# Five units of the second layer's input projection made ahead of a stage boundary and kept in PSUM

## The chip, the cores and the metric

The kernel runs on one core of a Trainium2 chip. The metric is the device time of one launch in microseconds (us); lower is better. The core has TensorE (PE, the matrix products), VectorE (DVE), ScalarE (ACT), GpSimd (POOL) and SyncE (SP, which here only issues transfers). Each runs its own list of instructions in order, and they wait for each other by semaphores. Matrix products are written to PSUM, which has 8 banks of 512 float32 numbers per partition; the other data lie in SBUF.

## The reference

One inference step of a two-layer decoder over 1024 prompt positions and 8 sequences of 8 new positions, 1088 columns in all. Layer 0 has mixers A and B, layer 1 the mixers C and D, and each layer ends with a SwiGLU block. The change lies where layer 0 ends and layer 1 begins:

```python
# end of layer 0
h = rmsnorm(x, norm_ffn_pre) * (1 + sc_f) + sh_f
f = swiglu(h, w_gate, w_up, w_down)          # (silu(h @ wg) * (h @ wu)) @ wd
x = x + g_f * rmsnorm(f, norm_ffn_post)
# start of layer 1
h = rmsnorm(x, norm_mix_pre) * (1 + sc_m) + sh_m
proj = h @ w_in
a, g, u, v = jnp.split(proj, [D_C, 2 * D_C, 2 * D_C + D_D], axis=-1)
hist = jnp.concatenate([conv_hist, a * jax.nn.sigmoid(g)], axis=1)
yc = causal_dwconv(hist, conv_w) + conv_b     # 31 taps per channel
yc = jax.nn.silu(layernorm(yc, ln_c_g, ln_c_b))
v = layernorm(v, ln_v_g, ln_v_b)
yd = chunk_spatial(u, v, w_sp, b_sp, chunk_rows)   # u * (tril(w_sp) @ v + b_sp)
y = jnp.concatenate([yc, yd], axis=-1) @ w_out
```

## The kernel before, in words

**Layout.** Activations lie with their features on the 128 partitions, as 8 blocks `d` or `k` of 128 features, and their 1088 columns in four quarters `q` of 272 (the last one has 208 prompt columns and the 64 new positions). A float32 product is made as three products: each operand is split into a high part (a copy in the type fp32r, by ScalarE) and a low part (the difference, by GpSimd or VectorE). `HS[:, 0]` and `HS[:, 1]` hold these parts of the input of the next projection. A weight tile of 1024 x 128 is loaded into a raw buffer by SyncE, copied to its high half by ScalarE (`to_hi`) and split by GpSimd (`to_lo`). A **unit** is one tile times one quarter: 24 products of 272 columns into one bank of PSUM.

**Stages.** The program is a row of stages with a barrier of all engines between them. In each, every engine's instructions are written out by hand in the order of a few loops over units; semaphores with counts tie them together. Of the stages two matter here.

`stage_tail` holds the output projection, the SwiGLU block and the residual additions of a layer. At its end, for layer 0 (`nxt` is set), the four quarters pass through: `close(q)` on TensorE (down products, and `add_f` summing squares of the result), `root_y` (ScalarE) and `invert_y` (VectorE) for the row scale, `scale_one(q, k)` (VectorE: f times gate and row scale; two operations in the last quarter), `add_x(1, q, i)` (GpSimd adds x from `x_part`, which SyncE reloads from `x_spill`, two buffers in turn), `square_x` (ScalarE), `sum_pair` and `fold` (VectorE), `sum_x` (TensorE), `root_x`, `invert_x`, `scale_x(q, k)` (VectorE), `scaled_high(q, k)` (ScalarE, two operations) and `low(q, k)` (GpSimd). The last three fill `HS` for layer 1 in a ring of four buffers `h_next`. The new positions are scaled and split by themselves at the very end (`samples_high`, `samples_low`). `sg` holds the gated products until the last `up`, whose low part raises `hid_lo`.

`stage_cd` is the C/D mixer. TensorE goes through the units `CD_UNITS`: numbers 0 to 7 are tiles `g` and `a` of the first 128 features, for quarters 0 to 3 in turn; 8 to 31 the other three pairs of tiles, four quarters each; then 9 token units (`v`, four tiles at once), 9 spatial units and 16 units `u`. A unit `n` goes to bank `n % 5` and waits until unit `n - 5` has been read: `g` by a sigmoid on ScalarE, `a` by `take_a` on VectorE, which multiplies it with the sigmoid's result. The causal convolution of group `j` is shared out: VectorE adds up `TAPS_V` of the 31 taps (`step`, in banks 6 and 7, two halves), ScalarE multiplies the others (`product`) and GpSimd adds them (`add`). They are spread over the units by the functions

```python
def steps_by(n):
    if n < 16:
        return max(0, min(steps_of[1], 4 * (n - 3)))
def products_by(n):
    if n < 16:
        return max(0, n - 7)
```

so VectorE takes its first four taps at its place `n == 4`, and ScalarE its first product at `n == 8`; both wait for the `take_a` of the quarters that they read. ScalarE makes the first four tiles' high halves before anything else. The spatial weights are turned by TensorE into banks 6 and 7 (`turn_spatial`, at unit 2), masked by VectorE (`mask`), repeated and summed (`row_sums`, unit 3), and set (`row_bias`), all ahead of the first tap.

## Time and profile before

| | |
|---|---|
| median of 3 runs | 3329.01 us (3327.11 to 3336.29) |
| the profiled execution, own time | 3332.6 us |
| its span in the trace | 3330.3 us |
| PE busy | 3086.1 us, 93% |
| DVE busy | 1459.2 us, 44% |
| ACT busy | 1073.5 us, 32% |
| POOL busy | 1064.2 us, 32% |
| mean granted TensorE clock | 0.963 of full speed |

The profile comes from one execution. Its times count from the start of its span; the time of the execution itself is 2.3 us longer than the span. An engine's share of busy time is a mean over stages in which different engines set the pace. The barrier that the change concerns lies at about 2092 us.

### The profile page before, as it was taken

The numbers are of one execution on the slowest core, as the hardware profiler recorded it, in microseconds if no ns is written. First come the engines' busy times: TensorE is split into PE (matmuls) and PEld (weight loads), VectorE is DVE, ScalarE is ACT, GpSimd is POOL, SyncE is SP. The second block draws the span as 40 slices with busy tenths as digits, with TensorE's granted clock in tenths as the row PEclk, the third lists the DMA queues.
The fourth block names the chain that finished last, engine by engine and source line by source line (L and its number), as shares of the span: only waits on it lengthen the run. The fifth ranks groups of instructions, "written<-read, shape, count | busy, mean of one in ns | idle before, by whom it ended". The sixth has DMA issues, their size and how long they took to land. (4 is left out here: it accounts for less than half of the span.)

```text
span 3330.3 us, 60742 instructions
## 1 busy us (share of the span) xinstructions
PE 3086.1 (93%) x24355; PEld 2794.2 (84%) x24355; DVE 1459.2 (44%) x2815; ACT 1073.5 (32%) x2114; POOL 1064.2 (32%) x684
## 2 busy tenths in 40 slices
PE   6999899899999889999999995788889999999997
PEld 4888566677766889999999994777889999999997
DVE  4332355344433563333333358586365333333335
ACT  4411146344443442111111125475553111111113
POOL 2410167333332543221221114477543222211212
PEclk8999989899999999999999997898899999999999
DMA  8555100355554332111111112211222111111103
GB/s 301 174 185 176 53 1 1 130 170 166 170 165 127 92 93 70 44 43 39 38 50 44 44 41 74 74 32 30 77 75 87 47 42 41 44 44 38 50 26 101
DMA packets 237865, 274.98 MB, mean 83 GB/s; under 512 B 12666, under 2 KB 185595, under 8 KB 237428
## 3 DMA queue, kind: packets, MB, share of 16 engines
q1 hardware_dynamic: 215532, 192.60, 18.5%
q0 software_dynamic: 20992, 75.51, 7.1%
q10 hardware_dynamic: 1168, 4.46, 0.4%
q8 instruction: 121, 1.98, 0.2%
q14 instruction: 52, 0.43, 0.0%
HBM read 248.64 MB, written 24.26 MB: 82 GB/s over the span
## 5 line engine op out<-in xcount | busy, mean ns | idle before, releaser
L511 PE MATMUL ps<-HS,w_ring 128*128 128x272 f32 x4992 | 646.9, 291 | 20.6 <-PEq L156 14.8
L511 PEld LDWEIGHTS ps<-HS,w_ring 128*128 128x128 f32 x4992 | 638.5, 190 | 22.2 <-POOLq L905 15.0
L511 PE MATMUL ps<-HS,w_split 128*128 128x272 f32 x4608 | 595.4, 291 | 14.8 <-POOL w_split L880 14.8
L511 PEld LDWEIGHTS ps<-HS,w_split 128*128 128x128 f32 x4608 | 589.5, 190 | 16.0 <-issue 12.9
L519 PE MATMUL ps<-hid,w_ring 128*128 128x272 f32 x4224 | 552.1, 291 | 2.9 <-DVE hid L1063 2.9
L519 PEld LDWEIGHTS ps<-hid,w_ring 128*128 128x128 f32 x4224 | 539.0, 189 | 7.0 <-DVE hid L1063 3.4
L880 POOL TENSOR_TENSOR w_ring<-w_raw,w_ring 128x1024 fp32r<-128x1024 f32 x92 | 219.4, 2397 | 828.5 <-ACT w_ring L621 828.5
L1138 DVE TENSOR_TENSOR Y<-Y,ps 128x272 f32<-128x272 f32 x576 | 252.2, 438 | 176.8 <-PE ps L519 176.8
L621 ACT ACTIVATE w_ring<-w_raw 128x1024 fp32r<-128x1024 f32 x92 | 94.6, 1053 | 471.0 <-PE ps L519 448.7
L1644 PEld LDWEIGHTS ps<-HS_in,w_split 128*128 128x128 f32 x1728 | 222.4, 191 | 27.6 <-issue 16.1
L1054 DVE TENSOR_TENSOR sg<-sg,ps 128x272 f32<-128x272 f32 x176 | 76.4, 437 | 385.3 <-ACT sg L708 385.2
L1644 PE MATMUL ps<-HS_in,w_split 128*128 128x272 f32 x1728 | 233.3, 294 | 9.2 <-DVE HS_in L1863 9.1
L880 POOL TENSOR_TENSOR w_split<-w_raw,w_split 128x1024 fp32r<-128x1024 f32 x46 | 111.2, 2419 | 359.4 <-ACT w_split L621 359.4
L2336 POOL DMA_INDIRECT pages_ckv<-cache_ckv_in,ckv_rows x128 | 120.1, 938 | 289.1 <-PE ps L2408 267.8
L712 ACT ACTIVATE hid<-sg 128x272 fp32r<-128x272 f32 x176 | 75.9, 431 | 413.3 <-DVE sg L1059 413.3
L1059 DVE TENSOR_TENSOR sg<-sg,ps 128x272 f32<-128x272 f32 x176 | 77.1, 438 | 257.0 <-PE ps L511 256.0
L708 ACT ACTIVATE sg<-ps 128x272 f32<-128x272 f32 x176 | 69.1, 397 | 332.8 <-PE ps L511 325.1
L2753 PE MATMUL ps<-HS,w_ring 128*128 128x272 f32 x1152 | 150.0, 293 | 22.3 <-POOL w_ring L2990 22.3
L2753 PEld LDWEIGHTS ps<-HS,w_ring 128*128 128x128 f32 x1152 | 148.0, 191 | 24.0 <-POOL w_ring L2990 23.1
L1063 DVE TENSOR_TENSOR hid<-sg,hid 128x272 fp32r<-128x272 f32 x176 | 115.3, 655 | 88.3 <-ACT hid L712 88.3
L897 POOL TENSOR_TENSOR Y<-Y,x_part 128x544 f32<-128x544 f32 x64 | 97.7, 1532 | 160.4 <-DVE Y L988 116.9
L2355 PEld LDWEIGHTS ps<-cst,pages_ckv 128*128 128x128 f32 x1024 | 112.9, 143 | 35.8 <-DMA pages_ckv<-cache_ckv_in,ckv_rows 29.1
(367 smaller groups left out, 4020.4 us busy)
## 6 DMA issues: line engine op xcount, KB each, us to landing
w_mod_half<-w_mod_in SPq DMA_DIRECT2D x40, 1024.0 KB, 6.9
w_raw<-w_ffn_gate_in SPq DMA_DIRECT2D x44, 512.0 KB
w_raw<-w_ffn_up_in SPq DMA_DIRECT2D x44, 512.0 KB
w_raw<-w_ffn_down_in SPq DMA_DIRECT2D x44, 512.0 KB
x_part<-x_spill SPq DMA_DIRECT2D x64, 272.0 KB, 3.0
x_spill<-Y SPq DMA_DIRECT2D x12, 1088.0 KB, 5.5
w_raw<-w_in_ab_in SPq DMA_DIRECT2D x18, 512.0 KB, 14.6
w_raw<-w_in_cd_in SPq DMA_DIRECT2D x16, 512.0 KB
```

The costliest lines, as they stand in the source:

```text
L511: ins = pe.matmul(bank(b), wt[:, a, k, :], HS[:, e, k, qs(q)], start=(k == 0 and j == 0), stop=(k == KD - 1 and j == 2))
L519: ins = pe.matmul(bank(b), slots[1 + f][:, a, d * P:(d + 1) * P], hid[:, e, f, qs(q)], start=(f == 0 and j == 0), stop=(f == 1 and j == 2))
L621: act.activation(slots[slot][:, 0, :], raw[u][:, :], ACT.Copy).then_inc(w_hi, 1)
L880: pool.tensor_tensor(slots[slot][:, 1, :], raw[u][:, :], slots[slot][:, 0, :].bitcast(F32), ALU.subtract).then_inc(w_lo, 1)
L897: pool.tensor_tensor(y, y, xc[:, 2 * (i % 2):2 * (i % 2) + 2, :], ALU.add).then_inc(x_added, 1)
L1059: dve.tensor_tensor(sg[:, qs(q)], sg[:, qs(q)], bank(b), ALU.mult).then_inc(gated, 1)
L1063: dve.tensor_tensor(hid[:, 1, f, qs(q)], sg[:, qs(q)], hid[:, 0, f, qs(q)].bitcast(F32), ALU.subtract).then_inc(hid_lo, 1)
L1138: dve.tensor_tensor(Y[:, d, qs(q)], Y[:, d, qs(q)], bank(b), ALU.add).then_inc(freed_dve, 1)
L1644: ins = pe.matmul(bank(n), wt[:, a, k, :], HS[:, e, k, qs(q)], start=(k == 0 and j == 0), stop=(k == KD - 1 and j == 2))
L2336: pool.indirect_dma_start(pg[g % NPB][:, e, :, :].rearrange("p a r -> p (a r)"), None, ckv_blocks, bass.IndirectOffsetOnAxis(c.ckv_rows[:, ...
L2355: ins = pe.transpose(CT_[e][:, k, j * P:(j + 1) * P], pg[u][:, e, j, k * P:(k + 1) * P], c.ident)
L2753: ins = pe.matmul(bank(n)[:, 0:Q], weights(t % 4, a, k), HS[:, e, k, qs(q)], start=(k == 0 and i == 0), stop=(k == KD - 1 and i == 2))
```

## The change

Five of the units of `stage_cd`, numbers 0 to 4 (`g` and `a` of the first features for quarters 0 and 1, and `g` for quarter 2), are made at the end of the first `stage_tail`, in banks 0 to 4, and left there over the barrier. For this the first two tiles of `w_in_cd` are loaded into `sg` one after the other once it is free, and split by ScalarE (`ahead_high`) and GpSimd (`ahead_low`) into slots 0 and 3 of the ring of weights; the order of slots in `stage_cd` becomes 0, 3, 2, 1. In `stage_cd` every engine counts these units and tiles as done and starts with tile 2 and unit 5. The spatial weights are turned in two halves at units 16 and 19, in bank 5, and set at 22 and 25. In the tail VectorE does all `scale_one` of the last quarter ahead of the `scale_x` of the one before it, half of which move behind the last `fold`; GpSimd does its additions of x ahead of the splits; and the last quarter's `HS` is made with one operation on ScalarE (`next_high`) and the split on VectorE (`low_next`). The second layer's tail has `nxt` unset and keeps its order.

```diff
--- before.py
+++ after.py
@@ stage_tail, SyncE
                 if nxt:
                     store_x(1, q)
+                if nxt and q == 1:
+                    sp.wait_ge(computed, U.final(3, 3) + 1)
+                    sp.wait_ge(hid_lo, HEND + 8)
+                    for u in range(2):
+                        if u:
+                            sp.wait_ge(a_lo, u)
+                        sp.dma_start(ahead_raw.rearrange("p (k n) -> p k n", k=KD), w_ahead[u]).then_inc(a_in[u], 16)
@@ stage_tail, TensorE
+            def ahead(n):
+                q, u = n // 2, n % 2
+                pe.wait_ge(a_lo, u + 1)
+                pe.wait_ge(h_lo, 33 + 8 * q + 8)
+                if n == 0:
+                    pe.wait_ge(freed_dve, U.END - U.P1)
+                wt = slots[ahead_slot[u]].rearrange("p a (k n) -> p a k n", k=KD)
+                for k in range(KD):
+                    for j, (a, e) in enumerate(((0, 0), (0, 1), (1, 0))):
+                        ins = pe.matmul(c.ps[:, n, 0:Q], wt[:, a, k, :], HS[:, e, k, qs(q)], start=(k == 0 and j == 0),
+                                        stop=(k == KD - 1 and j == 2))
+                ins.then_inc(ahead_done, 1)
+
             if nxt:
+                ahead(0)
                 sum_x(1, 2)
+                for n in range(1, 4):
+                    ahead(n)
                 sum_x(1, 3)
+                for n in range(4, CD_AHEAD):
+                    ahead(n)
+                pe.wait_ge(ahead_done, CD_AHEAD)
@@ stage_tail, ScalarE
+            def ahead_high(u):
+                act.wait_ge(a_in[u], 16)
+                act.activation(slots[ahead_slot[u]][:, 0, :], ahead_raw, ACT.Copy).then_inc(a_hi, 1)
+
                 if nxt:
                     root_x(1, q - 2)
+                if nxt and q == 3:
+                    ahead_high(0)
                 for d in range(KD):
                     square_f(q - 1, d)
                     if nxt:
                         scaled_high(q - 2, d)
+            def next_high(k):
+                layer, part, shift = nxt
+                act.wait_ge(h_made, 32 + 24 + k + 1)
+                act.activation(HS[:, 0, k, 3 * Q:NPR], h_next[k % 4][:, 0:QP], ACT.Identity,
+                               bias=c.mod[:, NM * layer + shift + k, 0:1]).then_inc(h_hi, 1)
+
+            if nxt:
+                ahead_high(1)
             for d in range(KD):
                 square_f(3, d)
@@
+            root_y(1, 3)
             if nxt:
                 root_x(1, 2)
-            root_y(1, 3)
-            if nxt:
-                scaled_high(2, 0)
                 for i in range(4):
-                    for k in range(2 * i + 1, min(2 * i + 3, KD)):
-                        scaled_high(2, k)
                     square_x(1, 3, i)
+                for k in range(4):
+                    scaled_high(2, k)
                 root_x(1, 3)
+                for k in range(4, KD):
+                    scaled_high(2, k)
                 for k in range(KD):
-                    scaled_high(3, k)
+                    next_high(k)
@@ stage_tail, GpSimd
+                if nxt and q == 1:
+                    ahead_low(0)
                 if nxt and q < 2:
                     for k in range(KD):
                         low(q, k)
+                if nxt and q == 1:
+                    ahead_low(1)
             for i in range(4):
-                if nxt:
-                    low(2, 2 * i)
-                    low(2, 2 * i + 1)
                 add_x(1, 3, i)
             if nxt:
                 for k in range(KD):
-                    low(3, k)
+                    low(2, k)
@@ stage_tail, VectorE
-                invert_x(1, 2)
             invert_y(1, 3)
             for k in range(KD):
-                if nxt:
+                scale_one(3, k)
+                if nxt and k == 5:
+                    invert_x(1, 2)
+            if nxt:
+                for k in range(4):
                     scale_x(2, k)
-                scale_one(3, k)
-            if nxt:
                 for i in range(1, 4):
                     sum_pair(1, 3, i)
                 fold(1, 3)
+                for k in range(4, KD):
+                    scale_x(2, k)
                 invert_x(1, 3)
-                for k in range(KD):
-                    scale_x(3, k)
+                make_next(0)
+                for k in range(1, KD):
+                    make_next(k)
+                    low_next(k - 1)
+                low_next(KD - 1)
@@ stage_cd
+CD_SLOT = (0, 3, 2, 1)
+CD_AHEAD = 5
@@ stage_cd, TensorE
-            for n in range(END):
-                if n == 2:
-                    turn_spatial()
-                if n == 3:
+            pe.sem_inc(computed, CD_AHEAD)
+            for n in range(CD_AHEAD, END):
+                if n in (TURN_AT, TURN_AT + 3):
+                    turn_spatial((n - TURN_AT) // 3)
+                if n == TURN_AT + 6:
+                    repeat_rows()
+                if n == TURN_AT + 9:
                     row_sums()
@@ stage_cd, ScalarE
-            for t in range(4):
-                to_hi(t)
+            act.sem_inc(w_hi, 2)
             for n in range(NU):
+                if n == 2:
+                    to_hi(2)
+                    to_hi(3)
@@ stage_cd, VectorE
-                if n == 2:
-                    mask()
-                if n == 3:
+                if n in (TURN_AT, TURN_AT + 3):
+                    mask((n - TURN_AT) // 3)
+                if n == TURN_AT + 6:
+                    set_rows()
+                if n == TURN_AT + 9:
                     row_bias()
```

`make_next` and `low_next` are one `scalar_tensor_tensor` of 128 x 208 each. `TURN_AT` is 16.

Three places in the instruction lists show what moved (line numbers are those of the file that a list belongs to). The first is TensorE across the boundary: `L540`/`L550` are the last `add_f`, `L534`/`L544` is `sum_x`, the branches are the barrier, `L2753`/`L2838` are column units, `L2784` and the lines up to `L2793` the products on the spatial weights. Before:

```order
L540 MATMUL ps<-square_12504,ones 128x272
L534 MATMUL ps<-squares_sum,ones 128x272 x2
L314 UNCONDITIONAL_BRANCH
L2742 UNCONDITIONAL_BRANCH
L2753 MATMUL ps<-HS,w_ring 128x272 x48
L2784 MATMUL ps<-cst,v_tok 128x128 x8
L2753 MATMUL ps<-HS,w_ring 128x272 x24
L2789 MATMUL ps<-w_sp_t,cst 64x64
L2793 MATMUL ps<-w_sp_t,ones 64x128 x8
L2753 MATMUL ps<-HS,w_ring 128x272 x696
```

Now, with `L627` the products of `ahead` and `L2871` the turning:

```order
L550 MATMUL ps<-square_12504,ones 128x272
L627 MATMUL ps<-HS,w_ring 128x272 x24
L544 MATMUL ps<-squares_sum,ones 128x272
L627 MATMUL ps<-HS,w_ring 128x272 x72
L544 MATMUL ps<-squares_sum,ones 128x272
L627 MATMUL ps<-HS,w_ring 128x272 x24
L314 UNCONDITIONAL_BRANCH
L2827 UNCONDITIONAL_BRANCH
L2838 MATMUL ps<-HS,w_ring 128x272 x264
L2871 MATMUL ps<-cst,v_tok 128x128 x4
L2838 MATMUL ps<-HS,w_ring 128x272 x72
```

One unit stands ahead of the second last `sum_x`, three ahead of the last and one behind it; the stage then begins with eleven units in a row.

The second place is ScalarE at the start of `stage_cd`: `L2846`/`L2939` is `to_hi`, `L2885`/`L2977` the sigmoid of a `g` unit. Before:

```order
L2840 UNCONDITIONAL_BRANCH
L2846 ACTIVATE w_ring<-w_raw_59 128x1024
L2846 ACTIVATE w_ring<-w_raw_60 128x1024
L2846 ACTIVATE w_ring<-w_raw_59 128x1024
L2846 ACTIVATE w_ring<-w_raw_60 128x1024
L2885 ACT_TABLE_LOAD
L2885 ACTIVATE Y<-ps 128x272 x4
```

Now:

```order
L2933 UNCONDITIONAL_BRANCH
L2977 ACT_TABLE_LOAD
L2977 ACTIVATE Y<-ps 128x272
L2939 ACTIVATE w_ring<-w_raw_59 128x1024
L2939 ACTIVATE w_ring<-w_raw_60 128x1024
L2977 ACTIVATE Y<-ps 128x272 x3
```

The first sigmoid stands ahead of all tiles, and the second behind two of them instead of four.

The third place is ScalarE in the tail, at the start of `close(2)`: `L713` is `root_x(1, 1)`, `L851` `square_f(2, d)`, and `L727` and `L728` are `scaled_high(1, d)`. Now:

```order
L713 ACT_TABLE_LOAD
L713 ACTIVATE row_scale_12502<-ps,eps 128x272
L855 ACTIVATE w_ring<-sg 128x1024
L851 ACTIVATE square_12503<-Y 128x272
L727 ACTIVATE HS<-w_raw_59,mod 128x272
L728 ACTIVATE w_raw_59<-w_raw_59,mod 128x272
```

The row `L855`, the copy of the first tile, is new; before, the squares followed the root at once.

## Rows read from the trace of the kernel before

**Rows 1.** The waits of TensorE over the whole run: total, times, longest.

```profile
PE ps L534 <- DVE squares_sum L1004: 39.0, 6, 23.8
```

**Rows 2.** Timeline of TensorE, 2046 to 2240: start, length, instructions, idle before.

```profile
2076.57 1.28 PE L534 MATMUL ps<-squares_sum,ones 128*128 128x272 f32 x2 [23.80 <-DVE squares_sum L1004]
2100.18 8.44 PE L2753 MATMUL ps<-HS,w_ring 128*128 128x272 f32 x48 [22.33 <-POOL w_ring L2990]
...
2117.52 87.96 PE L2753 MATMUL ps<-HS,w_ring 128*128 128x272 f32 x696
2217.65 22.70 PE L2763 MATMUL ps<-w_ring,HS 128*64 128x512 f32 x92 [12.18 <-POOL w_ring L2990]
```

**Rows 3.** Stretches: length, busy PE, PEld, DVE, ACT, POOL; clock, DMA.

```profile
2036.00:2048.00 12.00, 8.14 (x45) 6.58 (x45) 10.94 (x17) 4.32 (x10) 4.21 (x4) 1.00 0.18 48
2048.60:2092.70 44.10, 2.60 (x5) 1.01 (x4) 31.09 (x47) 20.83 (x41) 18.62 (x22) 0.52 0.24 76
...
2117.50:2205.50 88.00, 87.98 (x698) 87.74 (x696) 81.45 (x126) 58.07 (x144) 56.40 (x24) 0.99 0.13 38
```

**Rows 4.** Timeline of all engines, 2018 to 2024.5.

```profile
2019.49 0.44 DVE L1063 TENSOR_TENSOR hid<-sg,hid 128x272 fp32r<-128x272 f32 x1 [0.50 <-ACT hid L712]
...
2023.65 0.61 ACT L697 ACTIVATE HS<-w_raw,mod 128x272 fp32r<-128x272 f32 x1 [2.08 <-DVE w_raw L1042]
```

**Rows 5.** Timeline of all engines, 2092 to 2100.

```profile
2092.66 1.00 SPq L2715 DMA_DIRECT2D w_raw<-w_in_cd_in  x2
...
2096.64 1.06 ACT L2846 ACTIVATE w_ring<-w_raw 128x1024 fp32r<-128x1024 f32 x1 [5.91 <-DMA w_raw<-w_in_cd_in]
...
2098.45 1.06 ACT L2846 ACTIVATE w_ring<-w_raw 128x1024 fp32r<-128x1024 f32 x1 [0.75 <-DMA w_raw<-w_in_cd_in]
```

**Rows 6.** DMA issues, 2049 to 2059: size, median time to landing.

```profile
x_part<-x_spill SPq DMA_DIRECT2D x2, 272.0 KB, 5.8
```

**Rows 7.** Timeline of VectorE, 2049 to 2092.

```profile
2051.00 0.44 DVE L1004 TENSOR_TENSOR squares_sum<-squares_sum 128x272 f32<-128x272 f32 x1
...
2055.21 1.85 DVE L974 RECIPROCAL row_scale<-row_scale 128x272 f32<-128x272 f32 x1
...
2058.00 0.43 DVE L988 SCALAR_TENSOR_TENSOR Y<-Y,mod,row_scale 128x208 f32<-128x208 f32 x1
2058.35 0.22 DVE L991 TENSOR_TENSOR Y<-Y,row_scale 128x64 f32<-128x64 f32 x1
2058.49 0.43 DVE L1042 TENSOR_TENSOR w_raw<-Y,row_scale 128x272 f32<-128x272 f32 x1
...
2061.23 1.58 DVE L1042 TENSOR_TENSOR w_raw<-Y,row_scale 128x272 f32<-128x272 f32 x1
...
2071.50 0.71 DVE L999 TENSOR_TENSOR squares_sum<-squares_sum,w_raw 128x544 f32<-128x544 f32 x1
...
2091.01 0.69 DVE L1049 TENSOR_TENSOR HS<-x_part,HS 128x512 fp32r<-128x512 f32 x1 [3.31 <-POOL HS L902]
```

**Rows 8.** Timeline of GpSimd, 2049 to 2092.

```profile
2061.18 1.33 POOL L897 TENSOR_TENSOR Y<-Y,x_part 128x544 f32<-128x544 f32 x1
```

**Rows 9.** Timeline of VectorE, 2100 to 2123.

```profile
2113.49 1.67 DVE L3115 TENSOR_TENSOR w_sp_t<-ps,cst 128x128 f32<-128x128 f32 x8
2117.64 1.62 DVE L3121 TENSOR_SCALAR w_sp_s<-ps,cst 64x64 f32<-64x64 f32 x8 [2.48 <-PE ps L2793]
...
2121.36 0.44 DVE L3155 TENSOR_TENSOR Y<-ps,Y 128x272 f32<-128x272 f32 x1 [1.07 <-PE ps L2753]
```

**Rows 10.** Timeline of ScalarE, 2110 to 2200.

```profile
2124.39 0.40 ACT L2885 ACTIVATE Y<-ps 128x272 f32<-128x272 f32 x1 [11.08 <-PE ps L2753]
...
2190.25 0.41 ACT L2867 ACTIVATE glu_hist_s<-state_c 128x240 f32<-128x240 f32 x1 [2.54 <-DVE Y L3155]
```

**Rows 11.** Timeline of GpSimd, 2135 to 2375.

```profile
2215.16 2.35 POOL L2990 TENSOR_TENSOR w_ring<-w_raw,w_ring 128x1024 fp32r<-128x1024 f32 x1
...
2249.85 34.44 POOL L3002 TENSOR_TENSOR conv_part<-conv_part,tap_product 128x1007 f32<-128x1007 f32 x14 [3.52 <-ACT tap_product L2861]
```

More of the change, by code:

```diff
@@ L301, in close, with stage_tail @@
         return Units.SEAM + (8, 20, 32, 40)[q] + d
-def stage_tail(c, HS, l, w_out, spill, nxt, out, ring, split):
+def stage_tail(c, HS, l, w_out, spill, nxt, out, ring, split, w_ahead):
     nc = c.nc
@@ L1204, in _, with make_next, low_next @@
                 scale_one(2, d)
+            def make_next(k):
+                layer, part, shift = nxt
+                dve.wait_ge(h_lo, 33 + 24 + min(k - 3, 0))
+                if k >= 4:
+                    dve.wait_ge(n_lo, k - 3)
+                dve.scalar_tensor_tensor(out=h_next[k % 4][:, 0:QP], in0=Y[:, k, 3 * Q:NPR],
+                                         scalar=c.mod[:, NM * layer + part + k, 0:1], in1=rs[1][:, 0:QP],
+                                         op0=ALU.mult, op1=ALU.mult).then_inc(h_made, 1)
+            def low_next(k):
+                layer, part, shift = nxt
+                dve.wait_ge(h_hi, 33 + 24 + k + 1)
+                dve.scalar_tensor_tensor(out=HS[:, 1, k, 3 * Q:NPR], in0=h_next[k % 4][:, 0:QP],
+                                         scalar=c.mod[:, NM * layer + shift + k, 0:1],
+                                         in1=HS[:, 0, k, 3 * Q:NPR].bitcast(F32),
+                                         op0=ALU.add, op1=ALU.subtract).then_inc(n_lo, 1)
             if nxt:
@@ L2574, in _ @@
                                 ).then_inc(y_copied, 1)
[L2577 removed]
+CD_SLOT = (0, 3, 2, 1)
+CD_AHEAD = 5
+CD_TILES = [(kind, j) for j in range(KA) for kind in ("g", "a")] + [("v", s) for s in CD_SLOT] + [("u", s) for s in CD_SLOT]
 CD_COLUMN = {"a": 0, "g": DA, "u": 2 * DA, "v": 3 * DA}
@@ L2583 @@
             + [("v", t, 0) for t in TOKENS] + [("s", t, 0) for t in TOKENS]
-            + [("u", s, q) for q in range(4) for s in range(KA)])
+            + [("u", s, q) for q in range(4) for s in ((0, 3, 2, 1) if q < 3 else (0, 1, 3, 2))])
 CD_AT = {u: n for n, u in enumerate(CD_UNITS)}
@@ L2618, in last_use, with slot, last_u @@
         return NS - 1 if kind == "v" else at[kind, j, 3]
-    hi_after = {t: last_use(t - 4) for t in range(4, len(CD_TILES) + 2)}
+    hi_after = {t: last_use(t - 4) for t in range(4, len(CD_TILES) + 1)}
+    hi_after[len(CD_TILES) + 1] = last_use(len(CD_TILES) - 1)
     hi_slot = {t: hi_after[t] if t < 12 else NS for t in range(4, len(CD_TILES))}
+    def slot(t):
+        return CD_SLOT[t % 4] if t < len(CD_TILES) else t - len(CD_TILES)
+    def last_u(q):
+        return NU + KA * q + KA - 1
     def steps_by(n):
@@ L2726, in _ @@
             sp.dma_start(c.new_c_s[0, :, 0:H0 - NT, :], c.state_conv_c[0, :, NT:H0, :]).then_inc(stored, 16)
-            for t in range(2, 14):
+            for t in range(4, 14):
                 load(t)
@@ L2752, in columns @@
                     for i, (a, e) in enumerate(((0, 0), (0, 1), (1, 0))):
-                        ins = pe.matmul(bank(n)[:, 0:Q], weights(t % 4, a, k), HS[:, e, k, qs(q)], start=(k == 0 and i == 0),
+                        ins = pe.matmul(bank(n)[:, 0:Q], weights(slot(t), a, k), HS[:, e, k, qs(q)], start=(k == 0 and i == 0),
                                         stop=(k == KD - 1 and i == 2))
@@ L3025, in sum_three @@
                 pool.tensor_tensor(ysum[:, :], ysum[:, :], Y[:, 2, :], ALU.add).then_inc(ln_added, 1)
-            for t in range(4):
-                to_lo(t)
+            pool.sem_inc(w_lo, 2)
+            to_lo(2)
+            to_lo(3)
             for n in range(NU):
```

76 lines of the change are left out of this document (43 added, 33 removed).

## The prediction

> **What bounds the kernel now.** TensorE is busy for 93% of the span (the page's table above), so a change of order can win only where it stands idle. I read the list of waits first: its longest wait, 23.8 us, is one of the `sum_x` products, for VectorE [rows 1]. The timeline of TensorE puts this wait just ahead of the boundary between the first block's tail and the C/D stage, and the next one of 22.33 us right behind it [rows 2]. Between 2048.60 and 2092.70, the end of the tail, TensorE works 2.60 us of 44.10, VectorE 31.09 [rows 3]: VectorE sets the pace there. Behind the boundary nothing can run before the first weight tile is loaded and split. From 2117.50 to 2205.50 TensorE is busy 87.98 of 88.00 us, but VectorE also 81.45 [rows 3]. Then TensorE waits 12.18 us for the last weight tile's low half from GpSimd [rows 2]. So in the C/D stage the three other engines are nearly as loaded as TensorE. How early their chain of convolution taps starts counts for as much as how early TensorE does.
>
> **The change, part by part.** A unit is 24 products, 87.96 / 29 = 3.03 us [rows 2].
>
> *First tile in the tail.* SyncE may load it only when `sg` is free: 2019.49 + 0.44 = 2019.9 [rows 4]. The two loads behind the boundary were issued at 2092.66 and the first was being copied at 2096.64 [rows 5], 3.98 us later. So it lands at 2023.9, and the copy takes 1.06 us [rows 5]. ScalarE does this copy ahead of `square_f(2, 0)` and `scaled_high(1, 0)`. The latter ran at 2023.65 [rows 4]; now it follows at about 2025.4. Behind it in ScalarE's queue is all of `close(2)`'s squaring, for which TensorE's `add_f` waits, so this is 1.8 us on the path. If the store of x (1.1 MB, issued shortly before) holds the tile up, the nearest row is the 5.8 us of the pieces of x behind such a store [rows 6], and it costs 3.6. I take 1.8, since this store is issued ahead of the quarter's last two sums and the load only behind them.
>
> *Second tile, and GpSimd's two low halves.* The second load is issued at about 2027.6 and is copied at about 2036, in the gap in which ScalarE waits for the first sum of `close(3)`. That gap hides the copy; without it, it would cost 1.06. SyncE is held until the first low half is made, so the next pieces of x leave some 10 us later than before, yet before their use at 2041. I cost both at nothing.
>
> *The reordered drain.* The second last `sum_x` is ready at 2051.44 [rows 7], now 2053.2. Before, VectorE then made two reciprocals and alternated `scale_x(2, k)` with `scale_one(3, k)`, and GpSimd split `HS` between the additions of x. Now it does one reciprocal and the samples' gate (2055.21 to 2057.65, 2.4 us), eight `scale_one` at 0.49 (2058.00 to 2058.49), the other reciprocal at 1.9, and only four `scale_x` at some 0.4: 2.4 + 3.9 + 1.9 + 1.6 = 9.8 us with nothing beside them. GpSimd's four additions of 1.33 us [rows 8] slow it: a `scale_x` of 0.43 took 1.58 beside one [rows 7], so 1.15 each, 4.6. Three partial sums of 0.71 and a fold of 0.44 add 2.6 [rows 7]. 2053.2 + 9.8 + 4.6 + 2.6 = 2070.2 in place of 2076.57 [rows 2]. The Trainium skill says in "SBUF — State Buffer", section "Who interferes with whom", that a VectorE operation with two inputs in SBUF and a GpSimd operation exclude each other for a whole instruction; by that rule the four additions cost 5.3 instead of 4.6, and the time would be 0.7 later. The trace is near it: the 1.58 holds most of GpSimd's 1.33.
>
> *Last quarter.* From the last `sum_x` to the end of the tail it was 2076.57 to 2091.70, 15.1 us [rows 2, 7]. Making and splitting the last eight pieces on VectorE (`make_next`, `low_next`) replaces ScalarE's second pass and GpSimd's split. No row shows it in this place: eight pairs at 0.43 each are 6.9 us, against the 8.5 that the old form took; but the root must now wait for the other four `scale_x`, and GpSimd's eight splits fall beside VectorE's next work. The bounds are 1.6 shorter and 4.6 longer (four hindered operations); I take 1.7 longer, near the middle. The tail then ends at 2070.2 + 15.1 + 1.7 = 2087.0, 4.7 us earlier, with the five units run by TensorE in its idle time: 5 x 3.03 = 15.2 us, or 30.3 at half the clock, of the 41.5 that it idles. `ahead(0)` makes `sum_x(1, 2)` wait at most a unit, behind which VectorE still has `scale_one` to do.
>
> *Behind the boundary.* What counts is VectorE's first tap, which needs `take_a` of the second quarter: 2121.36 [rows 9]. Now its sums are in PSUM already, and it waits for ScalarE's sigmoid, which stands behind two copies of new tiles: 2098.45 + 1.06 + 0.40 = 2099.9 [rows 5, 10]. That is 21.4 us earlier, counted from an equal boundary. TensorE goes on with unit 5 after the first sigmoid, and VectorE asks for unit 5 eight taps later and for unit 7 sixteen taps later, so TensorE is not late.
>
> *The spatial weights.* Turning, masking and repeating them stood in front of the taps, 1.67 and 1.62 us on VectorE [rows 9]. Now they stand between taps, where VectorE has no slack: 3.3 us come back by unit 23. The bias rows after it hit no chain.
>
> *Who hands the lead on.* ScalarE waited 2.54 us for VectorE ahead of the third group's taps (2190.25, [rows 10]); its products feed GpSimd's additions, GpSimd's last split ended at 2217.51 [rows 11], and TensorE's token units began at 2217.65 [rows 2]. So they start earlier by what VectorE has gained, and so does the run of 14 additions behind them (34.44 us, [rows 11]). TensorE's own lead is larger and is lost in waits for banks: unit 5 started at 2117.52 + 2 x 3.03 = 2123.6, and now at about 2089.7 (the boundary at 2088.0, a table load and a sigmoid).
>
> Sum: -4.7 - 21.4 + 3.3 = -22.8 us. The profiled execution took 3332.6, so 3309.8 there; it stands 3.6 above the median of 3329.01, so the median becomes 3306.2.
>
> **The rivals.**
> A, the drain wins nothing: the reordering only pays for the late tile, and the tail ends where it did, or up to 2 us later. For it: the first tile's wait is new, and so is the root's. Against: four `scale_x` fewer ahead of the sum. -18.1 or -16.1: 3310.9 to 3313. If the taps too start later (slower loads), 3319.
> B, TensorE is the bound of the columns, not VectorE. For it: 87.98 of 88.00 busy. Against: VectorE's 81.45, and the 12.18 us wait. Then its own lead of 33.9 counts, less the products on the spatial weights that it still makes: from 2108.62 to 2117.52 it had a unit and these, with waits, so they are under 5.9 us [rows 2]. With 4 it is -29.9, 3299.1.
> C, no change: all that starts earlier only waits longer, because a chain that doesn't begin at the boundary sets the end of the stage. For it: 34.44 us of GpSimd's additions. Against: their first product hangs on VectorE's `take_a`, which moves too. 3329.
> D, slower: TensorE's clock. It showed 0.50 to 0.52 of full speed where TensorE idled, which is 1.2 of its 2.4 GHz, and 0.99 to 1.00 in the columns [rows 3]. Now TensorE will stop for a bank in nearly every unit. If it stays at 1.2 GHz, 26 units take 2 x 3.03 each, 157.6 us from 2089.7 to 2247, and the tokens start at least 29 us later than 2217.65: 3358. The last tile's copy and split (1.06 + 2.35) had to start by 2214.2 for tokens at 2217.65, so it decides once a unit takes more than (2214.2 - 2089.7) / 26 = 4.8 us on average, that is from six tenths of the stretch at 1.2 GHz. Against: from 2036 to 2048 it was busy 8.14 of 12.00 us, with short stops, at 1.00 [rows 3]. The Trainium skill names this case in "TensorE: Matmul & The Clock Gate", section "A second HAM failure mode: psum-queue depth-cycling": stops between groups of matmuls, made by waits for PSUM banks, can make the clock swing between its two levels. By that rule D would come; the stretch at 1.00 with a third of it idle speaks against.
>
> **How the numbers follow.** My forecast (19 to 27 us won) gets 0.50, A 0.20, B (27 to 32 won) 0.13, C 0.09, D or another loss 0.08. The predicted time is that of the forecast. A range of 3299 to 3320 holds the forecast, nearly all of A and most of B, and leaves out C and D. About 0.3%, 10 us, is what a measurement tells from no change: faster 0.83, same 0.09, slower 0.08.
>
> **What the changed profile would show.** The copy of the tile from `sg` in ScalarE near 2024, and `scaled_high(1, 0)` 1.8 us later than 2023.65. The last `sum_x` near 2070; the boundary's first load near 2088. Five units between `close(3)` and the boundary. The first tap 21 us earlier, counted from the boundary. Small waits of TensorE in the columns, and a clock near 1.00 there. The token units starting some 23 us earlier than 2217.65, and the same lead to the end. The prediction is wrong if the tile lands several us later, if VectorE waits for TensorE's turned weights, if the clock falls in the columns, or if the lead shrinks between the tokens and the output units.

## The result, and the profile after

The changed kernel took 3307.46 us (median of 4 runs, 3305.73 to 3308.59), the kernel before beside it 3329.82 us (4 runs, 3327.11 to 3336.29). The ratio is 0.993, with a 95% interval of 0.9912 to 0.9947: faster by 22 us, between 18 and 29. The forecast was 3306.0 with a range of 3299 to 3320.

The page of the changed kernel's profile begins so (busy time, share of the span, instructions):

```profile
span 3305.0 us, 60745 instructions
PE 3091.8 (94%) x24355; PEld 2800.5 (85%) x24355; DVE 1459.0 (44%) x2823; ACT 1070.1 (32%) x2106; POOL 1059.4 (32%) x676
```

TensorE does the same work; it waits less. Its list of waits (total, times, longest):

```profile
PE ps L544 <- DVE squares_sum L1054: 17.9, 5, 6.5
...
PE ps L2848 <- POOL w_ring L3084: 10.4, 1, 10.4
...
PE ps L627 <- POOL HS L946: 9.2, 1, 9.2
```

The two waits of 23.80 and 22.33 us [rows 2] are gone. What stands in their place is shown by TensorE's timeline, from the third quarter's `sum_x` to the token units (start, length, idle before and releaser in brackets; L627 are the units in the tail, L2838 the units behind the boundary, L2871 the turning of the spatial weights):

```profile
2012.18 0.73 PE L544 MATMUL ps<-squares_sum,ones 128*128 128x272 f32 x2 [1.99 <-DVE squares_sum L1054]
...
2044.28 3.38 PE L627 MATMUL ps<-HS,w_ring 128*128 128x272 f32 x24
2047.73 0.73 PE L544 MATMUL ps<-squares_sum,ones 128*128 128x272 f32 x2
2048.09 9.44 PE L627 MATMUL ps<-HS,w_ring 128*128 128x272 f32 x72
2064.05 1.27 PE L544 MATMUL ps<-squares_sum,ones 128*128 128x272 f32 x2 [6.51 <-DVE squares_sum L1054]
2074.49 5.01 PE L627 MATMUL ps<-HS,w_ring 128*128 128x272 f32 x24 [9.17 <-POOL HS L946]
2083.96 35.39 PE L2838 MATMUL ps<-HS,w_ring 128*128 128x272 f32 x264 [4.46 <-ACT Y L2977]
2119.19 0.60 PE L2871 MATMUL ps<-cst,v_tok 128*128 128x128 f32 x4
2119.55 9.36 PE L2838 MATMUL ps<-HS,w_ring 128*128 128x272 f32 x72
2134.41 1.09 PE L2871 MATMUL ps<-cst,v_tok 128*128 128x128 f32 x4 [5.50 <-DVE w_sp_t L3207]
...
2188.61 11.59 PE L2848 MATMUL ps<-w_ring,HS 128*64 128x512 f32 x38 [10.35 <-POOL w_ring L3084]
```

The reader is to see the five units: one (24 products) just ahead of the second last `sum_x`, three (72) inside the former wait ahead of the last one, and one (24) inside the former wait behind it. The last `sum_x` is at 2064.05, the sixth unit stands right behind the boundary, and two waits are left in the stage, 5.50 us at the turning and 10.35 us ahead of the tokens.

To compare traces, I count from the third quarter's `sum_x`: it stands ahead of everything that the change touches in time. It is at 2018.70 in the trace of before and at 2012.18 in that of after. The 6.5 us between them are early stages that the change doesn't edit; more traces say below what they are worth. Both kernels were profiled three times, "boundary" is SyncE's first load behind it, and the steps are differences between starts:

| us | before, 3 traces | after, 3 traces | shift of the mean, added up |
|---|---|---|---|
| to the second last `sum_x` | 32.8, 33.1, 34.8 | 35.6, 36.7, 35.2 | +2.3 |
| to the last `sum_x` | 57.9, 57.6, 59.3 | 51.9, 53.1, 51.5 | -6.1 |
| from there to the boundary | 16.1, 16.1, 16.1 | 18.2, 18.2, 18.2 | -4.0 |
| boundary to VectorE's first tap | 29.2, 30.9, 30.7 | 7.7, 7.8, 7.8 | -26.5 |
| first tap to the first token unit | 95.8, 95.8, 95.8 | 98.7, 98.8, 98.7 | -23.6 |
| from there to the end of the span | 1112.6, 1116.8, 1116.1 | 1116.4, 1117.7, 1117.0 | -21.8 |

### The profile page after: what moved, and what is told of

Its sections match the earlier page's. It is cut to its first block and busy times, and to the rows that moved or that the text cites. A ratio compares the mean times of both kernels' runs of the same rounds, so it can differ in the third digit from the quotient of the medians.

```text
span 3305.0 us, 60745 instructions
## 1 busy us (share of the span) xinstructions
PE 3091.8 (94%) x24355; PEld 2800.5 (85%) x24355; DVE 1459.0 (44%) x2823; ACT 1070.1 (32%) x2106; POOL 1059.4 (32%) x676
## 5 line engine op out<-in xcount | busy, mean ns | idle before, releaser
L521 PE MATMUL ps<-HS,w_ring 128*128 128x272 f32 x4992 | 644.8, 290 | 20.4 <-PEq L156 14.8
L521 PEld LDWEIGHTS ps<-HS,w_ring 128*128 128x128 f32 x4992 | 636.5, 190 | 22.0 <-POOLq L954 15.0
L941 POOL TENSOR_TENSOR Y<-Y,x_part 128x544 f32<-128x544 f32 x64 | 97.2, 1526 | 168.8 <-DVE Y L1038 115.7
L2838 PE MATMUL ps<-HS,w_ring 128*128 128x272 f32 x1032 | 138.5, 297 | 4.5 <-ACT Y L2977 4.5
L2428 PEld LDWEIGHTS ps<-cst,pages_ckv 128*128 128x128 f32 x1024 | 112.3, 142 | 34.8 <-DMA pages_ckv<-cache_ckv_in,ckv_rows 27.5
L2838 PEld LDWEIGHTS ps<-HS,w_ring 128*128 128x128 f32 x1032 | 136.1, 196 | 5.5 <-ACT Y L2977 4.7
```

The lines of the kernel that those rows point to most:

```text
L521: ins = pe.matmul(bank(b), wt[:, a, k, :], HS[:, e, k, qs(q)], start=(k == 0 and j == 0), stop=(k == KD - 1 and j == 2))
L941: pool.tensor_tensor(y, y, xc[:, 2 * (i % 2):2 * (i % 2) + 2, :], ALU.add).then_inc(x_added, 1)
L2428: ins = pe.transpose(CT_[e][:, k, j * P:(j + 1) * P], pg[u][:, e, j, k * P:(k + 1) * P], c.ident)
L2838: ins = pe.matmul(bank(n)[:, 0:Q], weights(slot(t), a, k), HS[:, e, k, qs(q)], start=(k == 0 and i == 0), stop=(k == KD - 1 and i == 2))
```

## The experiments

**First group, on one chip: is it the drain, the units, or TensorE's lead?** The changed kernel was run once more, then each half of the change alone, then all of it with three units ahead instead of five.

> The changed kernel itself, unaltered, to have its gain on the chip of the next three. Both traces taken from the last sum of the third tail quarter on (2018.70 before, 2012.18 after) give 18.8 us won; the medians gave 22.4. If the 6.5 us by which the changed kernel's trace was ahead at that point is chance, the gain here is nearer to 19 (ratio 0.994) and the stretch ahead of that point differs either way from run to run. If it is real, 22 to 25 again (ratio 0.993).

> The tail's new order (scale_one first, additions of x ahead of the splits, the last quarter split on VectorE) without any unit ahead and with the C/D stage of before. My theory: the two parts add up, the drain is worth 4.1 us measured at the boundary plus the 2.8 that the tile's copy had cost it, so 6 to 7 us faster than before (ratio 0.998), and the boundary 6 to 7 us earlier from the sum of the third quarter. Rival (the new order only repays the late tile): no change, the boundary where it was.

```diff
-                ahead(0)
                 sum_x(1, 2)
-                for n in range(1, 4):
-                    ahead(n)
                 sum_x(1, 3)
```

(and no loads, copies or splits of the two tiles in the tail; the C/D stage is that of before).

> Five units ahead and the rearranged C/D stage, with the tail's drain in the order of before. My theory: the boundary comes 2 to 3 us later than before (the tile's copy), the first tap 21.4 us earlier relative to it, 3.3 given back for the spatial weights: 13 to 16 us faster than before (ratio 0.9955). Rival (TensorE's lead counts): 5 units of 3.03 and the waits around them leave more, 20 us or more. Rival (the parts only work together): under 8 us.

The opposite: units, loads and the rearranged C/D stage as changed, but the last two quarters in the old order (`scale_x` alternating with `scale_one`, the last quarter split by ScalarE and GpSimd).

> The changed kernel with three units ahead instead of five; units 3 and 4 are made behind the boundary. My theory (VectorE's taps set the pace, TensorE's own lead is lost in waits for banks): the first tap waits for the second sigmoid, 7.3 us behind the boundary, by when unit 3 is done, so no change against the changed kernel, within 1 us. Rival (TensorE is the bound of the columns): 2 units of 3.03, 6.1 us slower than the changed kernel.

```diff
-CD_AHEAD = 5
+CD_AHEAD = 3
```

Measured, with before at 3334.18 us on this chip (the steps in the last three columns are those of the table above):

| kernel | median | ratio (95%) | to the last `sum_x` | boundary to tap | tap to tokens |
|---|---|---|---|---|---|
| after, again | 3312.1 | 0.9934 (0.9920 to 0.9947) | 53.1 | 7.8 | 98.8 |
| drain only | 3326.52 | 0.9976 (0.9966 to 0.9987) | 49.9 | 29.5 | 95.9 |
| units only | 3317.17 | 0.9954 (0.9940 to 0.9967) | 61.0 | 8.0 | 99.1 |
| three ahead | 3313.73 | 0.9948 (0.9934 to 0.9961) | 53.4 | 7.8 | 98.6 |

The changed kernel has its 22 us again. The drain alone is worth 8 us (4 to 11; 6 to 7 were expected), the units alone 15 us (11 to 20; as expected), together 23, against the 22 (18 to 27) of the whole: within these intervals the two halves add up. In the drain-only trace the last `sum_x` stands 8.4 us nearer than the mean of before, since no tile is in the way; with the units but the old drain it stands 2.7 us farther. So the reordering itself wins, and the tiles cost. Its timeline of TensorE has the old wait behind the boundary (24.57), and a shorter one ahead of it (15.04):

```profile
2065.05 1.27 PE L537 MATMUL ps<-squares_sum,ones 128*128 128x272 f32 x2 [15.04 <-DVE squares_sum L1033]
2090.90 8.68 PE L2808 MATMUL ps<-HS,w_ring 128*128 128x272 f32 x48 [24.57 <-POOL w_ring L3045]
```

With three units ahead TensorE has two units, 6 us, less of a lead. Its two waits in the stage:

```profile
2137.62 0.63 PE L2871 MATMUL ps<-cst,v_tok 128*128 128x128 f32 x4 [0.66 <-DVE w_sp_t L3207]
...
2191.78 8.46 PE L2848 MATMUL ps<-w_ring,HS 128*64 128x512 f32 x25 [12.66 <-POOL w_ring L3084]
```

Together they are 13.3 us instead of 15.9, the one at the turning nearly gone. But the first tap and the tokens are where they were: 178.0 us behind the third quarter's sum, 177.8 in the changed kernel on the same chip. If TensorE were the bound, the tokens would be 6 us later. Of these 6 us the shorter waits give back 2.6. TensorE also starts 1.6 us sooner behind the boundary, as it needn't wait there for the first sigmoid, and it spends some 2 us less at half its clock (granted 1.00 in the 8 us behind the turning, 0.64 in the changed kernel). That is rival B refuted: how far TensorE is ahead doesn't matter, VectorE's taps do.

**Second group: are the two steps that were given away really VectorE's?** The changed kernel loses 2.9 us between first tap and tokens, and its first tap waits 7.7 us behind the boundary.

> The changed kernel with TURN_AT at 24 instead of 16: turning, masking and repeating the spatial weights start eight units later, behind most of the taps. Theory: VectorE's chain of taps is what hands the lead on to the tokens, and the 2.9 us that the tokens lost between first tap and first token unit (98.68 against 95.81 us) are these instructions. Then the stretch from the first tap to the tokens is again about 95.8 us, and the time 2.5 to 3.3 us below that of the unchanged changed kernel, at a ratio of about 0.9925 to before. Rival (TensorE or ScalarE paces this stretch, or the longer stretch comes from the shifted phase of the engines against one another): the stretch stays at 98 to 99 us and the ratio at 0.9934.

```diff
-        TURN_AT = 16
+        TURN_AT = 24
```

> The changed kernel with ScalarE's copies of the two first new weight tiles moved from ahead of the second sigmoid to behind it. Theory (the first tap waits for that sigmoid alone, and everything up to the tokens hangs on the first tap): first tap 2.6 to 3.1 us behind the boundary instead of 7.7, tokens 4.7 us earlier against the boundary, ratio about 0.992. Rival 1 (TensorE's lead or the new tiles' transfers set the pace of the columns): first tap earlier, but the tokens no earlier, ratio 0.9934. Rival 2 (the lead is lost behind the tokens): tokens earlier, ratio 0.9934 all the same.

```diff
-                if n == 2:
+                if n == 4:
                     to_hi(2)
                     to_hi(3)
```

> The kernel before, unchanged, once more profiled. All traces with a changed tail or C/D stage reach the first block's third quarter 3 to 6.5 us earlier than the one trace of before, although nothing ahead of it was edited. Theory (the one trace of before was by chance slow in its early stages): the third quarter's sum at 2012 to 2016 instead of 2018.70, every later point at the same distance from it as in the first trace to within 0.5 us, and a span near 3326. Rival (something in the change makes the early stages shorter): the sum again at 2018 to 2019.

With the turning later the stretch from the first tap to the tokens is 95.9 us, the 95.8 of before: the theory's number, and the 2.9 us are the spatial weights between VectorE's taps. In this trace the same instructions of VectorE (0.88, 0.88 and 1.61 us, at 2164.89, 2176.12 and 2183.52) still stand ahead of the tokens at 2192.47; there they cost nothing. The ratio is 0.992 (0.9907 to 0.9934), some 5 us below that of after, though the intervals overlap; the trace carries the verdict here, not the timing.

With the sigmoid first, the timeline of all engines behind the boundary reads so:

```profile
2089.37 1.00 SPq L2800 DMA_DIRECT2D w_raw<-w_in_cd_in  x2
...
2090.68 0.69 ACT L2977 ACTIVATE Y<-ps 128x272 f32<-128x272 f32 x2
...
2092.01 0.81 DVE L3164 TENSOR_SCALAR ps<-Y,par 128x512 f32<-128x512 f32 x1
...
2093.48 1.06 ACT L2939 ACTIVATE w_ring<-w_raw 128x1024 fp32r<-128x1024 f32 x1 [2.11 <-DMA w_raw<-w_in_cd_in]
```

In the changed kernel the same engines read:

```profile
2082.63 0.57 SPq L2800 DMA_DIRECT2D w_raw<-w_in_cd_in  x1
...
2086.21 1.06 ACT L2939 ACTIVATE w_ring<-w_raw 128x1024 fp32r<-128x1024 f32 x1 [2.30 <-DMA w_raw<-w_in_cd_in]
2088.00 1.06 ACT L2939 ACTIVATE w_ring<-w_raw 128x1024 fp32r<-128x1024 f32 x1 [0.73 <-DMA w_raw<-w_in_cd_in]
2088.97 0.67 ACT L2977 ACTIVATE Y<-ps 128x272 f32<-128x272 f32 x2
2089.45 0.44 DVE L3250 TENSOR_TENSOR Y<-ps,Y 128x272 f32<-128x272 f32 x1 [4.99 <-ACT Y L2977]
2089.93 0.82 DVE L3164 TENSOR_SCALAR ps<-Y,par 128x512 f32<-128x512 f32 x1
```

The first tap (L3164) stands 2.64 us behind the boundary instead of 7.8, and the tokens 172.5 us behind the third quarter's sum, against 176.2 to 177.8 in the traces of after. From the boundary to the tokens are 101.3 us instead of 106.4 to 106.5, so the whole 5.1 us reach the tokens. The ratio is 0.9918 (0.9904 to 0.9932), as expected of the theory, though this interval too overlaps that of after. VectorE's 4.99 us of waiting had come from ScalarE standing ahead of a transfer whose result nobody needed yet.

The second trace of before differed from the first in ways that I had been about to put down to the change. From its first token unit to the end it needed 4.1 us more than in the first trace. The first pair of traces alone reads as if the changed kernel gave 3.7 us back behind the tokens (1116.4 against 1112.6); the kernel before does that by itself. But its third quarter's sum was at 2022.24, not at 2012 to 2016, so that part of the theory failed. So did the others: its first tap stood 30.9 us behind the boundary and not within 0.5 of 29.2, and its span was 3339.4 where about 3326 was expected.

**Third group: the tile's cost, everything together, and the control again.**

> The changed kernel with ScalarE's copy of the first weight tile in the middle of the third quarter's squaring (behind the fourth pair) instead of ahead of it, and GpSimd's low half of it behind the four pieces that it delayed. Theory (the copy's wait for the tile delays all of the squaring, 1.66 us, and the rest of the 2.7 to 3.9 us by which the second last sum comes late is TensorE at half its clock after the wait that this makes): the second last sum is 1.7 to 2.8 us earlier against the third quarter's sum (34 to 35 us instead of 36.7), the tail's end too, and the ratio 0.9925 to 0.993. Rival (the late sum has another cause, such as the low half on GpSimd or the store of x): the sum stays at 36 to 37 us, and the ratio at 0.9934.

```diff
-                if nxt and q == 3:
-                    ahead_high(0)
                 for d in range(KD):
                     square_f(q - 1, d)
                     if nxt:
                         scaled_high(q - 2, d)
+                    if nxt and q == 3 and d == 3:
+                        ahead_high(0)
```

> The changed kernel with all three edits together: the copy of the tile later, the second sigmoid ahead of the copies of the new tiles, the spatial weights turned eight units later. Theory (each takes its own term off the one chain of the tail's sums, first tap, taps and tokens): 5.3 + 2.9 + about 2 = 10 us less than the unchanged changed kernel, tokens at about 167 to 168 us behind the third quarter's sum instead of 176 to 178, ratio 0.990 to 0.991. Rival (with so much less on VectorE's chain, TensorE or the tiles' transfers become the bound): the tokens no earlier than 170 us, ratio 0.9915 or above.

> The kernel before, unchanged, a third profile, on the same chip as the next one. The first two traces of it differ from each other by 3.5 us at the third quarter's sum, by 1.7 in the wait for the first tap and by 1.6 in the last output units of the stage. Theory (the early stages' start differs by chance from execution to execution, and neither of these belongs to the change): its sum within 1.5 us of the next kernel's sum. Rival (the change makes the early stages shorter): 3 to 5 us later than it.

> The changed kernel, unchanged, a third profile, on the same chip as the third one of before. Theory: tokens 22 to 23 us earlier against the third quarter's sum than in before, and that sum within 1.5 us of before's. Rival: the sum 3 to 5 us earlier than before's, from early stages.

The later copy was a miss. The second last `sum_x` stands at 37.0 us, no earlier than the 35.2 to 36.7 of after, and the ratio is 0.9935 (0.9921 to 0.9949). Its GpSimd and VectorE timelines show what I had left out:

```profile
2028.48 2.39 POOL L952 TENSOR_TENSOR w_ring<-sg,w_ring 128x1024 fp32r<-128x1024 f32 x1 [0.18 <-ACT w_ring L855]
```

```profile
2028.67 2.50 DVE L1092 TENSOR_TENSOR w_raw<-Y,row_scale 128x272 f32<-128x272 f32 x1
```

A `scale` of 0.44 us took 2.50 beside GpSimd's low half of the tile, and ScalarE waited 1.14 us for it. With the 1.04 us of the copy itself, the last of the quarter's eight sums of squares was at 16.6 us instead of the 14.4 of before. The Trainium skill's "SBUF — State Buffer", section "Who interferes with whom", says that such a pair excludes each other for a whole instruction; by that rule, the trace agrees. The kernel with all three edits, below, has the same tail, and there nobody waited for the `scale` that was held (2.07 us): the last sum of squares came at 15.4, 1.0 us late by the copy alone. But the second tile's load now leaves later, ScalarE waits 1.09 us for it, and its copy, which was hidden in the changed kernel, costs another 1.0. So the later place saves the first wait and pays about as much elsewhere.

All three together gave 3301.38 us beside 3336.39 of before, ratio 0.9899 (0.9885 to 0.9913), tokens at 168.8 us: 2.64 us from boundary to tap and 95.9 from tap to tokens, both edits at their full price. The tokens are 0.8 us later than the 167 to 168 expected. The tile's term of about 2 us did not come, but the three traces of after differ by 1.6 us at this point, so the 0.8 proves nothing by itself.

The third pair of controls: the sum of before at 2019.82, that of after on the same chip at 2018.12, and tokens at 201.9 and 176.2. Both expectations were narrowly missed: the sums differ by 1.7 us, not by 1.5 at most, and the tokens by 25.8, not by 22 to 23. The rival's 3 to 5 us at the sum did not come either.

**The last run: are two edits enough?**

> The last combination without the later copy of the tile: second sigmoid ahead of the copies of the new tiles, spatial weights turned eight units later, the tail as in the changed kernel. The later copy gained nothing by itself (second last sum at 37.0 us behind the third quarter's, against 35.2 to 36.7 without it). Theory (these two edits carry the whole gain, 5.3 + 2.9 = 8.2 us): tokens at 167.5 to 169.5 us behind the third quarter's sum, ratio 0.9895 to 0.991, no different from all three. Rival (the later copy does help once the rest of the chain is shorter): tokens at 170 to 172, ratio 0.9915.

They are, as expected: 3295.63 us beside 3330.85 of before, ratio 0.9895 (0.9879 to 0.9912), tokens at 168.2. The interval of this kernel ends at 0.9912 and that of after in its five rounds begins at 0.9920 (in the four runs of the result it began at 0.9912), so it beats the changed kernel too. Its TensorE timeline:

```profile
2083.80 59.28 PE L2838 MATMUL ps<-HS,w_ring 128*128 128x272 f32 x456 [4.59 <-ACT Y L2977]
2142.93 0.60 PE L2871 MATMUL ps<-cst,v_tok 128*128 128x128 f32 x4
2143.28 9.33 PE L2838 MATMUL ps<-HS,w_ring 128*128 128x272 f32 x72
2154.01 0.63 PE L2871 MATMUL ps<-cst,v_tok 128*128 128x128 f32 x4 [1.40 <-DVE w_sp_t L3207]
...
2180.55 7.21 PE L2848 MATMUL ps<-w_ring,HS 128*64 128x512 f32 x24 [8.81 <-POOL w_ring L3084]
```

TensorE now runs 19 units (456 products) without a stop that the timeline splits at, and still waits 8.81 us for the last tile: there may be more to be had from VectorE's and GpSimd's chains, which no run here tried.

## Why the prediction was right, step by step

*The first tile in the tail, 1.8 us: right at its place.* The rows of ScalarE after:

```profile
2017.50 1.06 ACT L855 ACTIVATE w_ring<-sg 128x1024 fp32r<-128x1024 f32 x1 [2.77 <-DMA sg<-w_in_cd_in]
...
2018.79 0.60 ACT L727 ACTIVATE HS<-w_raw,mod 128x272 fp32r<-128x272 f32 x1
```

`scaled_high(1, 0)` (L727) is 6.61 us behind the third quarter's sum; before, 2023.65 - 2018.70 = 4.95 [rows 2, 4]. That is 1.66 later.

*The second tile and the low halves, nothing: right.* The second copy stands 17.2 us behind the third quarter's sum, where 17.3 was forecast, in ScalarE's gap. The prediction saw GpSimd's split only as a delay of SyncE's loads, and it can also hold VectorE: in the third trace of after a `scale` took 2.58 us beside a split of 2.37, and 2.61 in the kernel of the last run. But that was not what made the second last sum late: with the first tile's copy at this place, the four traces in which the `scale` was held have it at 35.2, 35.2, 36.4 and 36.7 us behind the third quarter's sum, the four in which it was not at 35.6, 36.7, 37.1 and 37.1.

*TensorE's clock in the tail, not in the sum: some 0.5 us.* The second last sum came 2.3 us later by the means, not 1.8, and at 35.2 to 37.1 us in all ten traces with the units. The rows show TensorE in the third quarter, before:

```profile
2025.14 0.72 PE L540 MATMUL ps<-square,ones 128*128 128x272 f32 x2 [0.72 <-ACT square L821]
2025.50 1.12 PE L519 MATMUL ps<-hid,w_ring 128*128 128x272 f32 x6
```

and after:

```profile
2018.93 0.73 PE L550 MATMUL ps<-square,ones 128*128 128x272 f32 x2 [2.55 <-ACT square L851]
...
2020.27 1.21 PE L550 MATMUL ps<-square,ones 128*128 128x272 f32 x2
2020.89 1.95 PE L529 MATMUL ps<-hid,w_ring 128*128 128x272 f32 x6
```

TensorE now waits 2.55 us for the squares that the copy made late, and behind this wait the same six products take 1.95 us instead of 1.12. From 6 to 12 us behind the third quarter's sum the granted clock was 1.00 in all three traces of before, and 0.72, 0.50 and 0.72 in those of after. In these three `scaled_high(1, 0)` was 1.7, 2.0 and 1.5 us late against the first trace of before, and the quarter's last sum of squares, at 16.3, 17.5 and 16.0 us instead of 14.4, was 1.9, 3.1 and 1.6 late: on average 0.5 more. From there to the second last `sum_x` both kernels need 19.0 to 19.2 us on average. The scatter of this step is larger than the term (32.8 to 34.8 in before itself), so its size stays rough.

*The reordered drain, the last sum 6.4 us earlier (2070.2 for 2076.57): right,* 6.1 by the means and 8.4 without the tiles. The sum of VectorE's pieces behind the second last one was 2070.2 - 2053.2 = 17.0 us; after has 2064.05 - 2047.73 = 16.3. The twelve pieces beside GpSimd's additions took 9.2 us where 5.5 was counted for them alone, so the additions cost 3.7 and not 4.6. One of them ran partly beside the reciprocal, which kept its length (1.84 us). The runs cannot tell the 0.7 us that the Trainium skill's rule would have added: the measured gap is on the other side of it.

*The last quarter, +1.7: right in its size, 2.1 us (18.2 - 16.1), but it was a choice between two bounds.* The reciprocal behind the last `sum_x`, before and after:

```profile
2078.40 1.85 DVE L1009 RECIPROCAL row_scale<-row_scale 128x272 f32<-128x272 f32 x1 [1.89 <-ACT row_scale L683]
```

```profile
2068.82 1.85 DVE L1059 RECIPROCAL row_scale<-row_scale 128x272 f32<-128x272 f32 x1 [0.60 <-ACT row_scale L713]
```

It stands 1.8 us behind the sum before and 4.8 after: VectorE has the four `scale_x` ahead of it, which wait three times some 0.65 us for GpSimd's splits, and then it waits 0.60 us for the root. That is 2.9 us lost. The new positions' three operations beside GpSimd's splits took 3.1 us instead of 2.2, another 0.9. The eight pieces themselves won 1.9 (6.7 for 8.5).

*The first tap, -21.4 from an equal boundary: right,* -22.5 by the means and -21.45 in the first pair of traces, whose rows it was worked out from. The cause given, ScalarE's sigmoid behind two copies, is the one that the sigmoid-first kernel removed.

*The spatial weights, +3.3: right,* 2.9, and gone when they were moved.

*The sum, -22.8: right.* The tokens are 23.6 us earlier, the span from the third quarter's sum on 21.8, the median 22.4. That it is so near is in part luck: the tail gave 0.7 us less than forecast, the first tap 1.1 more and the spatial weights cost 0.4 less. The 1.8 us lost behind the tokens are within the 4.1 by which the traces of before differ there.

*TensorE's lead "lost in waits for banks", with stops "in nearly every unit": wrong in form, with no effect on the sum.* From 2083.96 to 2188.61 are 104.65 us. The 27 units of it are 27 x 3.03 = 81.8, the products on the spatial weights 3.1, and the two waits 5.50 + 10.35 = 15.9, together 100.8; about 4 more is the first unit and the one behind the 5.50 wait at half the clock. Stops for banks need no term. The lead shrinks from some 33 us at unit 5 (104.9 us behind the third quarter's sum before, 71.8 after) to 22.5 at the tokens, in two waits, the first for VectorE's mask, which stands 16 units deep in VectorE's order.

The rivals. A (the drain wins nothing) fell with the drain-only kernel. B (TensorE the bound) fell with three units ahead. C (nothing changes) fell with the result. For the taps being late in case A, 3319, no working is given, and D counts 26 units where 5 to 31 are 27; neither changes the forecast. D (the clock in the columns) did not come: these stretches of after hold length, busy PE, PEld, DVE, ACT and POOL, the granted clock, and DMA:

```profile
2084.00:2088.00 4.00, 4.00 (x18) 4.00 (x19) 0.44 (x1) 1.06 (x1) 0.65 (x1) 0.50 1.18 308
2088.00:2130.00 42.00, 40.91 (x324) 40.68 (x323) 36.55 (x51) 24.00 (x54) 28.55 (x13) 0.99 0.32 91
2130.00:2134.00 4.00, 0.00 (x0) 0.00 (x0) 3.86 (x10) 0.50 (x3) 1.40 (x1) 0.88 0.31 88
2134.00:2142.00 8.00, 7.59 (x42) 7.62 (x43) 8.00 (x14) 8.00 (x24) 3.13 (x2) 0.64 0.08 23
2142.00:2178.00 36.00, 36.00 (x295) 35.46 (x293) 35.86 (x66) 27.99 (x69) 28.96 (x13) 1.00 0.11 32
```

The clock is at its lower level (1.2 GHz, 0.50) behind the boundary, and for a part of the 8 us behind the wait of 5.50 us (0.64); else it is at 2.4 GHz. By the Trainium skill's rule on depth-cycling ("TensorE: Matmul & The Clock Gate", section "A second HAM failure mode: psum-queue depth-cycling") frequent stops could make it swing; here the stops were two, not many, so the case that the rule speaks of did not arise and these columns say nothing on it.

**What stays open.** The third quarter's sum is at 2018.7, 2022.2 and 2019.8 in the three traces of before, and between 2012.2 and 2021.1 in the eleven others, 2016.0 on average, some 4 us earlier. On one chip the third pair differed by 1.7 us, and the kernel with all three edits was later than before by 1.3. On that chip alone the five changed kernels stand at 2018.4 on average and the two traces of before at 2021.0. Whether a part of the 4 us belongs to the changed program can't be told from these traces. The medians leave little room for it: the steps from the third quarter on make 21.8 us of their 22.4, and the profiled executions of before lay 2.8 to 3.4 us above the medians of their runs.

## What to carry to other kernels

When work is moved into an engine's idle time, price what the work needs from the other engines, not the engine's own gain: here TensorE got some 33 us of lead at its first unit behind the boundary, and at the tokens 22.5 were left, which is what VectorE's first tap had gained (25.4) less the 2.9 that its chain lost on the way. Behind a barrier, look at what the in-order engine does ahead of the instruction that starts the slowest chain: a copy that waits for a transfer, ahead of a sigmoid that waits for nothing, cost 5 us here and one line to move. And profile the old kernel more than once before explaining differences of 1 to 3 us between two traces.

## What the runs showed of the hardware that was not expected

The unchanged kernel has a scatter of its own of 2 us in a stretch of 33 us, and between its first and third trace it is TensorE's clock. From 6.4 to 23.2 us behind the third quarter's sum these two have every group of TensorE's products at the same place, to 0.02 us. In the tail's last quarter the same products (two sums of squares, L540) ran so in the first trace of before:

```profile
2041.89 0.72 PE L540 MATMUL ps<-square,ones 128*128 128x272 f32 x2 [1.21 <-ACT square L821]
2043.20 0.62 PE L540 MATMUL ps<-square,ones 128*128 128x272 f32 x2
```

and so in the third:

```profile
2043.01 1.28 PE L540 MATMUL ps<-square,ones 128*128 128x272 f32 x2 [1.21 <-ACT square L821]
2045.44 1.11 PE L540 MATMUL ps<-square,ones 128*128 128x272 f32 x2
2047.71 1.11 PE L540 MATMUL ps<-square,ones 128*128 128x272 f32 x2
```

The wait ahead of them is the same 1.21 us. The stretch of six microseconds around them shows the granted clock (third figure from the end), first in the one, then in the other:

```profile
2041.00:2047.00 6.00, 4.61 (x26) 3.73 (x26) 5.41 (x10) 3.02 (x8) 2.70 (x2) 1.00 0.34 93
```

```profile
2043.00:2049.00 6.00, 5.99 (x21) 5.30 (x22) 3.72 (x7) 2.38 (x6) 2.69 (x2) 0.51 0.34 92
```

The engine was at 2.4 GHz in the one and at 1.2 in the other, with the same work and the same waits in the 16 us ahead of it. The second last `sum_x` came at 32.8 us in the one and at 34.8 in the other. In the second trace the clock was at 0.50 only for some three microseconds (2043.24 to 2046.24), and the sum came at 33.1. Where TensorE works in short pieces between waits, a term of a microsecond or two is not to be settled by one trace.
